# Squares of the differential-attention heads moved from ScalarE to GpSimd, and the item drains from VectorE to ScalarE

## The chip, the cores and the metric

One core of a Trainium2 chip runs the whole program. The metric is the device time of one execution in microseconds (us); lower is better. The engines are TensorE (PE in the profile), VectorE (DVE), ScalarE (ACT), GpSimd (POOL) and SyncE (SP, which issues DMA transfers). Each engine runs its instructions in program order; they wait for each other by counting semaphores.

## The reference

The program is one inference step of a two-layer decoder trunk for a prompt of 512 tokens and 8 x 4 decode tokens. The part touched here belongs to layer 1, differential attention with 6 heads of 128 value channels. For each head two score matrices are made, each has its softmax, and

```python
a = p[:, :, 0] - lam * p[:, :, 1]
return jnp.einsum('bhqk,bkhe->bqhe', a.astype(v.dtype), v)
...
o = rmsnorm(o, p['subln'][j]) * (1.0 - lam_init)
```

So each row (query token) of each head's output `o` is divided by the root of the mean of its 128 squares. The sum of those 128 squares is the statistic that the change is about. `o` then goes through `w_out`, and the MLP follows.

## The kernel before

**The items.** The prompt attention of layer 1 is cut into items `("diff", h, i)`: head h (0 to 5) and query tile i (0 to 3, 128 query rows each); the number of a tile is k = 4h + i. Tile i sees (i+1)*128 keys. Between the 24 of them stand four `decode` items, each for two of the eight decode requests, so that the head loop has 28 steps. Counted from its start, the decode items are items 8, 12, 17 and 23; k = 0 to 7 are items 0 to 7, k = 8 to 10 are 9 to 11, k = 11 to 14 are 13 to 16, k = 15 to 19 are 18 to 22, and k = 20 to 23 are 24 to 27.

**The stages of an item n**, by engine:
- PE `scores(n)`: query by key matmuls into PSUM, then a bf16 mask matmul (L725, L728). A decode item has L738 and L745 and reads keys from `cache_tiles`.
- DVE `items_bias(n)`: row maximum (L1635), then the bias of the exponential (L1639).
- ACT `items_exp(n)`: two exponentials with row sums (L1169).
- DVE `items_weight(n)`: reciprocal of the sums (L1607), ratio (L1615), and the weighted difference of the two probability tiles (L1617, a scalar_tensor_tensor with two SBUF inputs).
- PE `turn(n)`: transposes (L768). ACT `items_copy(n)`: PSUM to SBUF (L1183). PE `mix(n)`: by the values, into PSUM bank 7 (L806; L816 for decode).
- DVE `items_drain(n)`: bank 7 times the reciprocal into `O[:, k, :]` ("attention_out", L1661). A decode item goes ACT copy (L1215), PE `decode_turn` (L836), DVE copies (L1667).
- POOL: clamps the tile into one of two halves of `SQ[:, 0]` (L2121). ACT `items_square(n)`: the square of the clamped tile and the square of the tile scaled by 2^-68, both with the row sum as accumulator (L1193, L1195), into `ss` and `ss_big`. The scaled sum serves to recognise rows too large for the plain one.

**The order.** It is written out by hand, one function `attention` per engine, and each is a loop over steps n:
- PE step n: `scores(n+2)`, `decode_turn(n-2)` if it is one, `turn(n)`, `mix(n-1)`. `mix(n)` waits for `copied` of n and for `drained` of n-1, since bank 7 is used by every item. At step 26 the transposes of heads 0 and 1 (`turn_head`, L852) stand ahead of `turn(26)`.
- DVE step n: `items_weight(n)`, `items_drain(n-2)`, `items_bias(n+2)`; at steps 14 and 18 also the low part of a weight tile (L1400).
- ACT step n: `items_exp(n+1)`, the decode copy of n-2, `items_copy(n)`, `items_square(n-3)`; at steps 14 and 18 the high part of a weight tile (L1021).
- Heads 0 to 3 are finished inside the loop: the means at DVE step 22, the square root at ACT step 23 (L1224, with a load of the activation table ahead of it and another one for the next exponential), and at DVE step 24 the factors (L1681, L1682) and four `scale_head` (L1687). ACT loads the Sqrt table again at step 27 (L1208).
- Heads 4 and 5 are finished behind the loop, where DVE works through `means`, `head_factors`, `scale_head` and `head_rest` (L1889) before PE can do the rest of the output projection (L978).

**The cache tiles.** SP loads keys and values of a decode item with four 384 KB transfers each (L497). The values of the next decode item wait for `mixed` of the one before, which `decode_turn` increments; the keys of the one after next stand behind them in SP's queue.

## Time and profile before

| | us |
|---|---|
| three runs | 1254.06, 1259.02, 1259.39; median 1259.02 |
| profiled execution, first to last instruction (its span) | 1251.9 |
| PE busy | 1177.3 (94%) |
| DVE busy | 849.9 (68%) |
| ACT busy | 516.0 (41%) |
| POOL busy | 432.9 (35%) |

For the profiled execution no time of its own is given beside the span. Busy times are sums over the whole span; the head loop is only the stretch from about 714 to 796 us of it, and has other shares. PE busy includes matmuls whose ends are modelled.

### The profile page before, as it was taken

How to read it: one execution, taken by the hardware profiler on the slowest of the kernel's cores; microseconds unless marked ns; L12 is line 12 of the kernel's file. 1: busy time of each engine (PE TensorE's matmuls, PEld its weight loads, DVE VectorE, ACT ScalarE, POOL GpSimd, SP SyncE). 2: the span in 40 equal slices, each digit the busy share in tenths (PEclk: the TensorE clock that was granted, in tenths of full speed). 3: DMA queues.
4: the chain of work that ended last, by engine and by line, in shares of the span. 5: the costliest groups of instructions: out<-in, count | busy, mean ns of one | idle time of the engine just before them, and what ended most of it. 6: DMA issues, size and time to landing. Idle time of an engine off the chain costs nothing.

```text
span 1251.9 us, 23862 instructions
## 1 busy us (share of the span) xinstructions
PE 1177.3 (94%) x9338; PEld 1124.8 (90%) x9338; DVE 849.9 (68%) x1332; ACT 516.0 (41%) x1013; POOL 432.9 (35%) x332
## 2 busy tenths in 40 slices
PE   6998998999999999999999998798999999999996
PEld 6877888899999999999899855697999999999996
DVE  7667568776776767556643887667967767677634
ACT  7445334443343434334422277534434434333321
POOL 3363014453443444221036210011634434444312
PEclk9999999999999999999999999999899999999997
DMA  7632321322323223423255276022223232232302
GB/s 286 215 119 67 132 85 51 118 85 99 104 68 118 85 75 118 146 68 102 96 146 138 94 261 243 1 84 61 94 87 113 72 118 85 69 117 85 103 33 72
DMA packets 46229, 134.96 MB, mean 108 GB/s; under 512 B 4178, under 2 KB 6354, under 8 KB 45490
## 3 DMA queue, kind: packets, MB, share of 16 engines
q1 hardware_dynamic: 45026, 125.39, 30.0%
q0 software_dynamic: 1104, 8.15, 2.1%
q8 instruction: 74, 1.21, 0.4%
q14 instruction: 25, 0.20, 0.0%
HBM read 123.15 MB, written 7.03 MB: 104 GB/s over the span
## 4 chain that ended last, share of the span: by engine, by line
PE 70%; DVE 13%; ACT 6%; POOL 5%; issue 3%; DMA 2%; SPq 0%; ACTq 0%; DVEq 0%; POOLq 0%
PE psum L640 30%; PE psum L622 23%; PE psum L556 11%; DVE weights_split L1400 3%; ACT weights_split L1021 2%; ACT squares L1033 1%; DVE inv_rms L1421 1%; DMA rotated<-keys 1%; DMA rotated<-projected 1%; DVE residual L1425 1%; POOL projected L2089 1%; POOL projected L2090 1%; PE psum L711 1%; POOL rotated L2088 1%; PE psum L806 1%
## 5 line engine op out<-in xcount | busy, mean ns | idle before, releaser
L640 PE MATMUL psum<-operand_b,weights_split 128*128 128x272 f32 x1536 | 196.8, 289 | 2.2 <-DVE weights_split L1489 1.9
L640 PE MATMUL psum<-operand_a,weights_split 128*128 128x272 f32 (+1 forms) x1536 | 196.6, 289 | 1.9 <-DVE weights_split L1489 1.9
L640 PEld LDWEIGHTS psum<-operand_b,weights_split 128*128 128x128 f32 x1536 | 195.1, 190 | 2.6 <-DVE weights_split L1489 2.2
L640 PEld LDWEIGHTS psum<-operand_a,weights_split 128*128 128x128 f32 x1536 | 195.0, 190 | 2.2 <-DVE weights_split L1489 2.2
L556 PE MATMUL psum<-operand_b,weights_split 128*128 128x272 f32 x1344 | 177.0, 292 | 6.3 <-DVE weights_split L1400 6.1
L556 PEld LDWEIGHTS psum<-operand_b,weights_split 128*128 128x128 f32 x1344 | 171.3, 190 | 12.2 <-DVE weights_split L1400 8.0
L556 PE MATMUL psum<-operand_a,weights_split 128*128 128x272 f32 (+1 forms) x948 | 128.4, 294 | 20.6 <-DVE weights_split L1400 16.6
L556 PEld LDWEIGHTS psum<-operand_a,weights_split 128*128 128x128 f32 x948 | 122.1, 193 | 27.3 <-issue 16.5
L1400 DVE TENSOR_TENSOR weights_split<-weights_raw,weights_split 128x1024 fp32r<-128x1024 f32 (+1 forms) x66 | 86.4, 1309 | 45.9 <-ACT weights_split L1021 45.9
L1971 POOL TENSOR_TENSOR mem_keys<-weights_raw 128x512 f32<-128x512 f32 x28 | 39.7, 1419 | 212.4 <-DMA weights_raw<-in_weights 212.4
L1021 ACT ACTIVATE weights_split<-weights_raw 128x1024 fp32r<-128x1024 f32 (+1 forms) x66 | 66.3, 1004 | 91.8 <-PE psum L556 90.6
L1489 DVE TENSOR_TENSOR weights_split<-weights_raw,weights_split 128x1024 fp32r<-128x1024 f32 x64 | 91.7, 1435 | 9.2 <-ACT weights_split L1092 9.2
L1501 DVE TENSOR_TENSOR residual<-psum,residual 128x544 f32<-128x544 f32 x63 | 45.6, 723 | 67.8 <-PE psum L640 67.7
L622 PE MATMUL psum<-mixed_tokens,up_weights_a 128*128 128x272 f32 x672 | 89.2, 289 | 0.0
L622 PEld LDWEIGHTS psum<-mixed_tokens,up_weights_a 128*128 128x128 f32 x672 | 86.4, 188 | 0.0
L1993 POOL TENSOR_TENSOR operand_b<-staging,operand_b 128x544 fp32r<-128x544 f32 x32 | 53.6, 1692 | 82.3 <-ACT staging L1097 82.2
L1955 POOL TENSOR_TENSOR squares_sum<-squares_sum,squares 128x544 f32<-128x544 f32 (+1 forms) x35 | 47.7, 1364 | 98.7 <-ACT squares L1033 98.1
L1993 POOL TENSOR_TENSOR operand_a<-staging,operand_a 128x544 fp32r<-128x544 f32 x32 | 53.7, 1694 | 81.0 <-ACT staging L1097 80.9
L1477 DVE TENSOR_TENSOR up_weights_a<-weights_raw,up_weights_a 128x512 fp32r<-128x512 f32 x56 | 80.4, 1435 | 1.2 <-ACT up_weights_a L1079 1.2
L1092 ACT ACTIVATE weights_split<-weights_raw 128x1024 fp32r<-128x1024 f32 x64 | 67.1, 1048 | 17.2 <-PE psum L640 17.2
L1495 DVE TENSOR_TENSOR residual<-psum,residual 128x544 f32<-128x544 f32 x64 | 46.0, 718 | 37.0 <-PE psum L640 36.9
L1079 ACT ACTIVATE up_weights_b<-mem_values 128x512 fp32r<-128x512 f32 x28 | 17.7, 632 | 109.8 <-POOL mem_values L1984 109.8
(288 smaller groups left out, 2065.9 us busy)
## 6 DMA issues: line engine op xcount, KB each, us to landing
weights_raw<-in_weights SPq DMA_DIRECT2D x186, 512.0 KB, 3.7
cache_tiles<-in_page_k SPq DMA_DIRECT2D x16, 384.0 KB, 4.0
cache_tiles<-in_page_v SPq DMA_DIRECT2D x16, 384.0 KB, 4.1
cache_tiles<-in_mem_k SPq DMA_DIRECT2D x8, 512.0 KB, 4.5
cache_tiles<-in_mem_v SPq DMA_DIRECT2D x8, 512.0 KB, 5.1
residual<-in_x SPq DMA_DIRECT2D x1, 2176.0 KB, 12.8
rotated<-projected POOLq DMA_DIRECT2D x4, 408.0 KB, 7.2
rotated<-keys POOLq DMA_DIRECT2D x4, 408.0 KB, 7.0
```

The lines of the kernel that those rows point to most:

```text
L556: mm = pe.matmul(ps[:, 2 * (j % PS) + hf, 0:n], w(wr), act[:, ar, k, hf * n:(hf + 1) * n], start=(q == 0 and wr == 0 and ar == 0), stop=(q ...
L622: mm = pe.matmul(up_bank(UP_BANK[q]), up_split(q)[:, wr, lo_of(kk)], up_tokens(h2, q, ar, kk), start=(kk == 0 and wr == 0 and ar == 0), st ...
L640: mm = pe.matmul(ps[:, bank, 0:part.stop - part.start], w(wr), hidden[:, ar, 4 * (c % 2) + kk, part], start=(kk == 0 and wr == 0 and ar == 0),
L1021: act.activation(split[:, s % HL, 0, 0:n], raw[:, s, 0:n], ACT.Copy).then_inc(weight_hi, 1)
L1092: act.activation(split[:, d % HL, 0, :], raw[:, u % RAW, :], ACT.Copy).then_inc(weight_hi, 1)
L1400: dve.tensor_tensor(split[:, s % HL, 1, 0:n], raw[:, s, 0:n], split[:, s % HL, 0, 0:n].bitcast(F32), ALU.subtract).then_inc(weight_lo, 1)
L1477: ins = dve.tensor_tensor(at[:, 1, :], up_source(q, u % RAW), at[:, 0, :].bitcast(F32), ALU.subtract)
L1489: dve.tensor_tensor(split[:, d % HL, 1, :], raw[:, u % RAW, :], split[:, d % HL, 0, :].bitcast(F32), ALU.subtract).then_inc(weight_lo, 1)
L1495: dve.tensor_tensor(halves(X[:, k, :]), ps[:, 0:2, 0:HALF], halves(X[:, k, :]), ALU.add)\
L1501: dve.tensor_tensor(halves(X[:, k, :]), ps[:, 2:4, 0:HALF], halves(X[:, k, :]), ALU.add)\
L1955: pool.tensor_tensor(sq_sum[:, 0:cols], a, SQ[:, k % 2, 0:cols], ALU.add).then_inc(sq_summed, 1)
L1993: pool.tensor_tensor(hidden[:, 1, k, :], T[:, c, :], hidden[:, 0, k, :].bitcast(F32), ALU.subtract).then_inc(hid_lo, 1)
```

## The change

ScalarE now drains all `diff` items: `head_drain(n-2)` stands in ACT's step n between `items_exp(n+1)` and `items_copy(n)`, and behind the Sqrt table load of step 27. DVE drains only the decode items. For k = 0 to 19 POOL does the squares in five instructions per tile: clamp; scale by 2^-68; square of both at once (128x256); and two folding additions, of 2x64 and of 2x32 columns. The last leaves 2x32 partial sums per tile in `SQ[:, 1]`, and DVE adds them up for a whole head with one tensor_reduce of 2x4x32 elements, five steps behind the head's last item. For k = 20 to 23 (head 5) ACT still squares. `EARLY_DONE` grows by one, which puts the means of heads 0 to 3 at DVE step 23, the square root at ACT step 24, and factors and `scale_head` at DVE step 25.

```diff
+SQUARED = QT * (HEADS - 1)
...
+        stat_pairs = tiny[:, 16:160].rearrange("p (q k) -> p q k", q=2)
+        def square_pair(k):
+            return SQ[:, 0, 2 * P * (k % 2):2 * P * (k % 2) + 2 * P].rearrange("p (q c) -> p q c", q=2)
+        def head_sums(h):
+            at = 2 * P * (h % 2)
+            return SQ[:, 1, at:at + 2 * P].rearrange("p (q i c) -> p q i c", q=2, i=QT)
...
-        EARLY_DONE = FIRST_HEAD + ITEMS[FIRST_HEAD:].index(("diff", EARLY_HEADS - 1, QT - 1)) + 3
+        EARLY_DONE = FIRST_HEAD + ITEMS[FIRST_HEAD:].index(("diff", EARLY_HEADS - 1, QT - 1)) + 4
+        HEAD_LAST = [FIRST_HEAD + ITEMS[FIRST_HEAD:].index(("diff", h, QT - 1)) for h in range(HEADS)]
...
 ScalarE
             def items_square(n):
                 kind, a, i = ITEMS[n]
+                if kind == "diff" and QT * a + i >= SQUARED:
...
+            def head_drain(n):
+                kind, a, i = ITEMS[n]
                 if kind == "diff":
-                    k = QT * a + i
-                    act.wait_ge(clamped, k + 1)
-                    if k:
-                        act.wait_ge(squared, k)
-                    own.step(act.activation(SQ[:, 1, 0:P], SQ[:, 0, k % 2 * P:k % 2 * P + P], ACT.Square,
-                                            accum_out=ss[:, k:k + 1]))
-                    act.activation(SQ[:, 1, P:2 * P], O[:, k, :], ACT.Square, scale=BIG,
-                                   accum_out=ss_big[:, k:k + 1]).then_inc(squared, 1)
+                    act.wait_ge(mixed, n + 1)
+                    act.wait_ge(weighted, n + 1)
+                    act.activation(O[:, QT * a + i, :], ps[:, 7, 0:P], ACT.Copy, scale=coef[:, n % SLOTS, 0:1])\
+                       .then_inc(drained, 1)
...
+                    if n0 <= n - 2 < n1:
+                        head_drain(n - 2)
...
 VectorE
-                elif kind == "diff":
-                    s = n % SLOTS
-                    ins = dve.tensor_scalar(O[:, QT * a + i, :], ps[:, 7, 0:P], coef[:, s, 0:1], None, ALU.mult)
...
-                    if n - 2 >= n0:
+                    if n - 2 in DECODE:
                         items_drain(n - 2)
...
+                    if n - 5 in HEAD_LAST[:HEADS - 1]:
+                        h = HEAD_LAST.index(n - 5)
+                        dve.wait_ge(squared, QT * h + QT)
+                        dve.tensor_reduce(stat_pairs[:, :, QT * h:QT * h + QT], head_sums(h), AX.X, ALU.add)\
+                            .then_inc(head_summed, 1)
                     if n == EARLY_DONE + 1:
-                        dve.wait_ge(squared, EARLY)
+                        dve.wait_ge(head_summed, EARLY_HEADS)
...
-            dve.wait_ge(squared, QT * HEADS)
+            dve.wait_ge(head_summed, HEADS - 1)
+            dve.wait_ge(last_squared, QT * HEADS - SQUARED)
...
 GpSimd
                     k = QT * a + i
+                    pair = square_pair(k)
                     pool.wait_ge(drained, n + 1)
...
-                    pool.tensor_scalar(SQ[:, 0, k % 2 * P:k % 2 * P + P], O[:, k, :], CLAMP, -CLAMP, ALU.min, ALU.max)\
-                        .then_inc(clamped, 1)
+                    ins = pool.tensor_scalar(pair[:, 0, :], O[:, k, :], CLAMP, -CLAMP, ALU.min, ALU.max)
+                    if k >= SQUARED:
+                        ins.then_inc(clamped, 1)
+                    else:
+                        own.step(ins)
+                        own.chain(pool.tensor_scalar(pair[:, 1, :], O[:, k, :], BIG, 1.0, ALU.mult, ALU.mult))
+                        own.chain(pool.tensor_tensor(pair, pair, pair, ALU.mult))
+                        own.chain(pool.tensor_tensor(pair[:, :, 0:64], pair[:, :, 0:64], pair[:, :, 64:P], ALU.add))
+                        if a >= 2 and i == 0:
+                            pool.wait_ge(head_summed, a - 1)
+                        pool.tensor_tensor(head_sums(a)[:, :, i, :], pair[:, :, 0:32], pair[:, :, 32:64], ALU.add)\
+                            .then_inc(squared, 1)
```

## Rows read from the trace of the kernel before

**Rows 1.** Stretches: length; busy of PE, PEld, DVE, ACT, POOL; PEclk; DMA share; GB/s

```profile
714.00:723.00 9.00, 6.10 (x39) 3.24 (x38) 7.50 (x23) 6.85 (x25) 4.78 (x17) 1.00 0.99 350
...
728.00:741.00 13.00, 12.39 (x165) 8.16 (x164) 9.65 (x30) 10.04 (x45) 1.17 (x4) 1.00 0.53 186
741.00:754.00 13.00, 11.15 (x86) 6.89 (x82) 9.64 (x38) 9.07 (x38) 0.88 (x3) 1.00 0.74 243
754.00:767.00 13.00, 11.68 (x118) 6.57 (x116) 10.06 (x28) 9.52 (x38) 1.17 (x4) 1.00 0.73 244
767.00:780.00 13.00, 11.57 (x115) 8.15 (x117) 11.68 (x45) 8.87 (x39) 1.17 (x4) 1.00 0.76 273
780.00:790.00 10.00, 6.27 (x47) 3.20 (x48) 8.15 (x24) 8.39 (x26) 0.38 (x2) 1.00 0.04 16
```

**Rows 2.** Chain of waits, 706 to 812: start, duration, what

```profile
720.84 0.26 DVE attention_out L1661
...
745.54 3.81 DMA cache_tiles<-in_page_v
...
764.49 0.39 ACT squares L1193 x2
764.88 0.29 ACT squares L1195 x2
```

**Rows 3.** Groups by line and shape, 706 to 800: busy us, mean ns, idle before

```profile
L1661 DVE TENSOR_SCALAR attention_out<-psum,tiny 128x128 f32<-128x128 f32 x24 | 8.3, 347 | 2.8 <-PE psum L806 2.5
...
L1193 ACT ACTIVATE squares<-squares 128x128 f32<-128x128 f32 x24 | 7.2, 301 | 0.2
...
L1193 ACT ACTIVATION_READ_ACCUMULATOR squares<-squares 128x1 f32 x24 | 4.6, 192 | 0.0
...
L1635 DVE TENSOR_REDUCE tiny<-psum 128x2 f32<-128x256 f32 x6 | 2.5, 417 | 0.5 <-PE psum L728 0.5
...
L1183 ACT ACTIVATE staging<-psum 128x128 f32<-128x128 f32 x6 | 1.7, 277 | 2.8 <-PE psum L768 2.8
```

**Rows 4.** Groups of POOL by shape, whole span

```profile
L2121 POOL TENSOR_SCALAR squares<-attention_out 128x128 f32<-128x128 f32 x24 | 7.0, 292 | 68.5 <-DVE attention_out L1661 65.6 <-ACT squares L1195 2.9
...
L1955 POOL TENSOR_TENSOR squares_sum<-squares_sum,squares 128x544 f32<-128x544 f32 x29 | 43.1, 1488 | 96.7 <-ACT squares L1033 96.7
...
L1955 POOL TENSOR_TENSOR squares_sum<-squares_sum,squares 128x256 f32<-128x256 f32 x6 | 4.6, 764 | 2.0 <-ACT squares L1033 1.4
```

**Rows 5.** Timeline of DVE and POOL, 211 to 222 (MLP); last, L1617's ns minimum/median/maximum

```profile
212.40 1.77 DVE L1477 TENSOR_TENSOR up_weights_a<-weights_raw,up_weights_a 128x512 fp32r<-128x512 f32 x1
...
214.73 0.67 DVE L1477 TENSOR_TENSOR up_weights_a<-mem_keys,up_weights_a 128x512 fp32r<-128x512 f32 x1
...
211.57 2.06 POOL L1980 TENSOR_TENSOR weights_raw<-weights_raw 128x512 f32<-128x512 f32 x1
...
L1617 DVE SCALAR_TENSOR_TENSOR probs_heads<-probs_heads,tiny x15: 352/485/752, 718.0 to 788.9; 128x256 f32<-128x256 f32 x5, 128x384 f32<-128x384 f32 x4, 128x128 f32<-128x128 f32 x3, 128x512 f32<-128x512 f32 x3
```

**Rows 6.** Timeline of the end of the head loop, 782 to 794

```profile
782.08 0.24 DVE L1681 RECIPROCAL tiny<-tiny 128x16 f32<-128x16 f32 x1
...
782.57 2.50 DVE L1687 TENSOR_TENSOR attention_out<-attention_out,tiny 128x512 f32<-128x512 f32 x4
...
785.52 0.50 ACT L1215 ACTIVATE staging<-psum 128x384 f32<-128x384 f32 x1
...
788.44 0.17 DVE L1607 RECIPROCAL tiny<-tiny 128x2 f32<-128x2 f32 x1
...
790.03 0.17 DVE L1607 RECIPROCAL tiny<-tiny 128x2 f32<-128x2 f32 x1 [0.20 <-ACT staging L1169]
...
790.72 1.28 ACT L1208 ACT_TABLE_LOAD   x1
...
792.12 0.58 ACT L1183 ACTIVATE staging<-psum 128x512 f32<-128x512 f32 x1
...
793.21 1.13 PE L806 MATMUL psum<-values,staging 128*128 128x128 f32 x8 [0.54 <-DVE attention_out L1661]
```

More of the change, by code:

```diff
@@ L277, in build @@
         mixed, drained = sem("mixed"), sem("drained")
-        squared, clamped = sem("squared"), sem("clamped")
+        squared, clamped, last_squared = sem("squared"), sem("clamped"), sem("last_squared")
+        head_summed = sem("head_summed")
         new_mixed, new_added = sem("new_mixed"), sem("new_added")
@@ L969, in _ @@
             turn_head(3)
-            pe.wait_ge(squared, QT * HEADS + 1)
+            pe.wait_ge(last_squared, QT * HEADS - SQUARED + 1)
             pe.matmul(ps[:, 1, 0:NS], ones[:, :], SQ[:, 0, 0:NS], start=True, stop=True)
@@ L1187, in items_square @@
                 kind, a, i = ITEMS[n]
-                if kind == "diff":
-                    k = QT * a + i
-                    act.wait_ge(clamped, k + 1)
-                    if k:
-                        act.wait_ge(squared, k)
-                    own.step(act.activation(SQ[:, 1, 0:P], SQ[:, 0, k % 2 * P:k % 2 * P + P], ACT.Square,
-                                            accum_out=ss[:, k:k + 1]))
-                    act.activation(SQ[:, 1, P:2 * P], O[:, k, :], ACT.Square, scale=BIG,
-                                   accum_out=ss_big[:, k:k + 1]).then_inc(squared, 1)
+                if kind == "diff" and QT * a + i >= SQUARED:
+                    k = QT * a + i
+                    act.wait_ge(clamped, k - SQUARED + 1)
+                    if k > SQUARED:
+                        act.wait_ge(last_squared, k - SQUARED)
+                    own.step(act.activation(SQ[:, 1, 2 * P:3 * P], square_pair(k)[:, 0, :], ACT.Square,
+                                            accum_out=ss[:, k:k + 1]))
+                    act.activation(SQ[:, 1, 3 * P:4 * P], O[:, k, :], ACT.Square, scale=BIG,
+                                   accum_out=ss_big[:, k:k + 1]).then_inc(last_squared, 1)
+            def head_drain(n):
+                kind, a, i = ITEMS[n]
+                if kind == "diff":
+                    act.wait_ge(mixed, n + 1)
+                    act.wait_ge(weighted, n + 1)
+                    act.activation(O[:, QT * a + i, :], ps[:, 7, 0:P], ACT.Copy, scale=coef[:, n % SLOTS, 0:1])\
+                       .then_inc(drained, 1)
             def head_high(h):
@@ L1358, in _ @@
             act.wait_ge(sub_mean, 2)
-            act.wait_ge(squared, QT * HEADS)
+            act.wait_ge(head_summed, HEADS - 1)
+            act.wait_ge(last_squared, QT * HEADS - SQUARED)
             own.step(act.activation(SQ[:, 0, 0:NS], small[0], ACT.Square))
             act.activation(SQ[:, 1, 0:NS].rearrange("p (h t) -> p h t", h=MIXT), Z[:, 0:MIXT, PROMPT:TOK], ACT.Square,
-                           scale=BIG).then_inc(squared, 1)
+                           scale=BIG).then_inc(last_squared, 1)
             act.wait_ge(sub_mean, 3)
@@ L2117, in _ @@
                     k = QT * a + i
+                    pair = square_pair(k)
                     pool.wait_ge(drained, n + 1)
-                    if k >= 2:
+                    if k >= SQUARED + 2:
+                        pool.wait_ge(last_squared, k - SQUARED - 1)
+                    elif k >= 2:
                         pool.wait_ge(squared, k - 1)
-                    pool.tensor_scalar(SQ[:, 0, k % 2 * P:k % 2 * P + P], O[:, k, :], CLAMP, -CLAMP, ALU.min, ALU.max)\
-                        .then_inc(clamped, 1)
+                    ins = pool.tensor_scalar(pair[:, 0, :], O[:, k, :], CLAMP, -CLAMP, ALU.min, ALU.max)
[10 more added lines that the diff above has]
+                            .then_inc(squared, 1)
             sum_squares(R_MLP1)
```

## The prediction, written before the changed kernel was run

> **What bounds the kernel now.** I read first the busy time by stretch of the head loop [rows 1], then its chain of waits [rows 2], then the costs of the instructions that go or come [rows 3, 4], and last the timeline of the loop's end [rows 6], since the change moves work between steps there. Outside this loop the change touches nothing.
>
> In the six stretches shown PE is busy for 12.39 of 13 us at best and 6.27 of 10 at worst; its idle time is 2.90 + 0.61 + 1.85 + 1.32 + 1.43 + 3.73 = 11.8 us [rows 1]. PE is therefore the nearest to a bound, no edit on DVE or ACT can be worth more than these 11.8 us, and the reader should look for what ends each of those idle times. ACT has 6.85 to 10.04 us busy in 9 to 13, DVE 7.50 to 11.68: neither is full over a whole stretch but the two take turns in holding PE up. DVE's drain stands in the chain for 0.26 us at 720.84 and four times more behind (at 756.50, 758.60, 773.64, 792.71); ACT's squares stand in it with 0.39 + 0.29 = 0.68 us at 764.49 [rows 2]. The stretch from 741 to 754 is held by something else: the value tiles of the second decode item, the last of which needs 3.81 us to land, at 749.35 [rows 2]. Their issue waits for the transpose of the first decode item, and the keys of the third are issued behind them, so from 741 to about 754 a faster ACT or DVE gives nothing, for all of PE's 1.85 idle us.
>
> **What goes.** From DVE 24 drains of 0.347 us, 8.3 us [rows 3]. From ACT the squares of 20 tiles: two activations of 0.30 and two reads of the accumulator of 0.19 each, 0.98 us busy a tile, 20 x 0.98 = 19.7 us [rows 3], of which 0.68 us a tile shows in the chain because they overlap [rows 2]. Following the chain, what it gives back is: 0.26 at 720.84; 0.25 at 756.50 (there PE has the third decode item's scores to finish, so the squares ahead at 752.9 give nothing more); 0.26 at 758.60; 0.68 at 764.49, where ACT's squares, its weight tile and its exponential stand in line; 0.26 at 773.64. Sum 1.7 us. The other 19 pairs of squares lie beside time in which ACT waits for PE's transposes anyway.
>
> **What ACT gets.** 24 drains. The trace has no PSUM-to-SBUF activation with a scale of this shape; the plain copy of 128x128 takes 0.277 us [rows 3], and DVE's own drain, which has the scale, 0.347; I take 0.30, with these as the ends, 6.6 to 8.3 us in all. Inside the loop they stand ahead of `items_copy(n)`, which mostly waits for PE: nothing, except at the end (below). `mix(n-1)` and POOL wait for them.
>
> **What DVE gets.** Five reductions of 256 elements, 0.417 us by the nearest row, which reads PSUM [rows 3]; 2.1 us. They stand behind `items_bias(n+2)` at steps 8, 12, 18, 23 and 27, where DVE next waits for ACT or PE; the second lies in the stretch held by the DMA. I take 0, with 2.1 as the other end. Each waits for POOL: queued behind it is `items_weight(n+1)`, and PE's transposes wait for that.
>
> **What POOL gets.** Per tile a clamp and a scale of 0.292, a square of 128x256 at 0.764, and folds of 128 and 64 elements. From 256 to 544 elements the addition grows from 0.764 to 1.488 us, 2.5 ns an element [rows 4]; so 0.44 and 0.28. Sum 2.07 us, and with four hand-overs from one instruction to the next, some 0.07 us each as an estimate, 2.35. Tiles 0 to 7 are drained within 15.8 us, one every 2.25 us, so POOL is at the loop's own pace there and about 1 us behind after eight. The reduction of a head comes five steps behind its last item, three steps (some 7 us) behind its drain. POOL is not late; a wait there costs 0.
>
> **The shared resource.** While POOL's L1980 ran until 213.63, a DVE subtraction with two SBUF inputs, started at 212.40, took 1.77 us; the same shape with POOL idle took 0.67 at 214.73 [rows 5]. So such a DVE instruction waits for the end of POOL's. In the head loop every diff item has one, L1617, of 0.35 to 0.75 us [rows 5], and the small L1639 too. Now POOL is busy there for about 1 us in 13 [rows 1]; afterwards for most of the time. An instruction that arrives at random while POOL works waits for half the running one, weighted by length: (2 x 0.29² + 0.76² + 0.44² + 0.28²) / (2 x 2.07) = 0.25 us. In the chain stand seven L1617 before 780, of which I find five at a time when POOL will be at work: 5 x 0.25 = 1.2 us. The ends: 0, if POOL always finds itself the one that waits, and 48 x 0.25 = 12 us if all of both kinds were in the chain.
>
> The Trainium skill, "SBUF — State Buffer", section "Who interferes with whom", says that a DVE instruction with two SBUF inputs contends with a GpSimd instruction that reads SBUF, and that the second to issue is fully blocked until the first ends. By that rule the trace agrees: 1.77 against 0.67 us. A rule of proportional sharing would leave the weights late by a tenth of a microsecond and the sum some 0.7 us lower; the full block speaks against the change, because the order of issue and not the priority decides.
>
> **The end of the loop.** Here something is moved, and this decides the sign. Factors and four `scale_head` take from 782.08 to 784.99, 2.9 us [rows 6]. Before, they stand at step 24, in the time when DVE waits for ACT's decode copy (785.52) anyway, which comes behind the square root, its two table loads and two exponentials. Afterwards they stand at step 25, behind `items_bias(27)`, directly ahead of `items_weight(26)`. The decode copy comes at the same time as before: what ACT saves in squares it loses in waiting for `turn(24)` before it can start the square root. So `items_weight(26)` starts not at 788.44 but at 791.35. Before, 0.20 us of wait for the exponential lay ahead of `items_weight(27)` at 790.03 [rows 6]; now it follows at 791.35 + 1.13 = 792.48: 2.45 us later. PE's transposes of heads 0 and 1 lie beside that and give nothing.
>
> ACT adds to this. Its Sqrt table load at 790.72 lies before in the wait for `turn(27)`, and the copy starts at 792.12 [rows 6]. Now it starts only when the copy of item 26 is through, 793.6, and it and its activation last 1.4 us; then drain 25 (0.3) and the copy of 27. `mix(26)` waits for drain 25 until 795.3. Drain 26 stands behind copy 27 and the squares of tile 20 (0.8), and ends at 796.9; `mix(27)` starts at 797.0 instead of 793.21 [rows 6]: 3.8 us later, the above 2.45 included. Behind the loop drain 27, two pairs of squares and `head_high` on ACT make DVE's means 0.4 us later still. Sum 4.2 us. What follows is a line of DVE work and then PE without gaps: the delay stays.
>
> **Sum.** -1.7 + 1.2 + 4.2 = +3.7 us: the span goes from 1251.9 to 1255.6. The span is all that is known of the profiled execution; it is 7.1 us under the median of the runs shown, 1259.02, whose own spread is 5.3 us. I add the 3.7 to the median: 1262.7.
>
> **Rivals.**
> - (A) The relief of ACT carries further than the chain shows, since with ACT early the exponentials, and so the weights, run ahead. For it: PE's idle time of 2.90, 1.32 and 1.43 us in stretches without the DMA. Against it: DVE is 7.5 of 9 and 11.7 of 13 us busy in two of them. It would give all 5.7 us of these and no blocking; with the 4.2 us of the end, -1.5: 1257.5. If `scale_head` also found cover, 2.45 less: 1255.
> - (B) Blocking decides. If POOL, slowed by DVE in turn (0.35 to 0.75 us once a tile, to about 2.9 us against a pace of 2.25), keeps a backlog, L1617 meets a busy POOL every time and DVE becomes the bound from its first tile: it loses 0.3 us a drain and gains 0.5 us a tile, and the reductions begin to wait. 20 tiles x 0.25 to 0.5 in the chain are 5 to 10 us: -1.7 + 7 + 4.2 = +9.5, 1268.5. It decides from about 2.7 us of POOL per tile. Against it: the pauses of POOL at each decode item (7 to 9 us between drains) clear the backlog.
> - (C) The end costs nothing, because ACT, free of squares, does the square root before `turn(24)` would stop it: -0.5 us in all, 1258.5. Against it is only ACT's order, which is fixed.
>
> **How the numbers follow.** Forecast 0.50, its own range 1260 to 1266; A 0.17, B 0.18, C 0.15. The range of eight in ten, with the runs' own scatter of 5 us: 1255 to 1269.5. Half a per cent, 6.3 us, is what a measurement of this kernel can tell from no change. Beyond it on the slow side lie most of B and a tail of the forecast: 0.24. On the fast side only a lucky A with scatter: 0.10. The rest 0.66.
>
> **What would show it.** Right: four L1687 directly ahead of L1617 with 384 keys, DVE without a gap there; the table load of L1208 behind the last but one copy and not in a wait; PE's gap ahead of the last two `mix` longer; L1617 with a maximum above 0.9 us; 741 to 754 of unchanged length; POOL at 2.3 to 2.6 us a tile. Wrong: no waits of DVE for POOL and a loop up to the first square root shorter by more than 3 us (A), or POOL above 2.7 us a tile and DVE waiting at the reductions (B), or the decode copy 2 us earlier (C).

## The result, and the profile after

| | us |
|---|---|
| changed kernel, median of five runs | 1261.2 (1260.36 to 1263.95) |
| kernel before beside it, median of six runs | 1254.2 (1253.0 to 1259.39) |
| ratio, with its 95% interval | 1.0046 [1.0028, 1.0063] |
| profiled execution of the changed kernel | 1263.95, span 1262.2 |

A sixth run of the changed kernel, 1902 us, was disturbed and is left out. The ratio compares runs taken side by side: the change costs 0.46%, 5.8 us, with an interval from 3.5 to 7.9; forecast were 3.7, just inside it. The profiled execution is the slowest of the five, so its span exaggerates: 10.3 us over the span before.

The stretches of the changed kernel's head loop, with the columns of [rows 1]:

```profile
714.00:723.00 9.00, 6.02 (x32) 3.36 (x34) 6.97 (x20) 7.36 (x27) 5.71 (x19) 0.89 0.98 337
...
728.00:741.00 13.00, 11.97 (x118) 8.01 (x117) 10.47 (x27) 8.16 (x29) 9.16 (x22) 1.00 0.53 187
...
767.00:780.00 13.00, 11.24 (x115) 6.20 (x111) 10.02 (x29) 8.04 (x24) 7.78 (x17) 1.00 0.60 210
...
790.00:796.00 6.00, 2.66 (x14) 2.29 (x15) 4.44 (x14) 2.91 (x9) 0.63 (x1) 0.73 0.00 0
796.00:805.00 9.00, 6.86 (x29) 5.52 (x27) 2.71 (x8) 4.25 (x15) 0.59 (x2) 0.50 0.01 3
805.00:815.00 10.00, 10.00 (x51) 9.94 (x52) 6.37 (x18) 5.69 (x19) 0.29 (x1) 0.59 0.00 0
```

ACT has less to do (8.16 against 10.04 us in 728 to 741, 8.04 against 8.87 in 767 to 780) and POOL much more (9.16 against 1.17), as the change says. PE did not profit: its idle time in 767 to 780 is 1.76 us against 1.43 [rows 1]. New is the column PEclk in the last three rows: the granted clock is 0.73, 0.50 and 0.59 there. The kernel before has in its own last stretches:

```profile
790.00:796.00 6.00, 4.77 (x39) 4.26 (x38) 2.33 (x7) 5.58 (x21) 1.08 (x4) 1.00 0.01 3
796.00:805.00 9.00, 7.17 (x56) 6.71 (x54) 8.69 (x22) 4.71 (x11) 0.00 (x0) 1.00 0.00 0
```

The timeline of the changed kernel's end of the loop, answering to [rows 6] (start, duration; in brackets the idle time before it and who ended it). L1711 is now the `scale_head` line, L1634 the reciprocal of `items_weight`, L1666 was L1639, L1644 was L1617, L821 was L806, L851 was L836 (`decode_turn`), L1241 was L1215, L867 is `turn_head`, L859 the matmuls of the new tokens, L1219 is ACT's new drain:

```profile
786.29 1.28 ACT L1250 ACT_TABLE_LOAD   x1
...
787.91 1.28 ACT L1184 ACT_TABLE_LOAD   x1
...
790.34 0.49 ACT L1241 ACTIVATE staging<-psum 128x384 f32<-128x384 f32 x1
...
790.88 0.55 PE L851 MATMUL psum<-constants,staging 128*128 128x128 f32 x3 [2.21 <-ACT staging L1241]
...
793.16 0.16 DVE L1666 SCALAR_TENSOR_TENSOR tiny<-tiny 128x2 f32<-128x2 f32 x1
793.24 0.24 DVE L1705 RECIPROCAL tiny<-tiny 128x16 f32<-128x16 f32 x1
...
793.72 2.59 DVE L1711 TENSOR_TENSOR attention_out<-attention_out,tiny 128x512 f32<-128x512 f32 x4
...
794.56 1.94 PE L867 MATMUL psum<-constants,attention_out 128*128 128x128 f32 x8 [1.96 <-DVE attention_out L1711]
...
796.24 0.15 DVE L1634 RECIPROCAL tiny<-tiny 128x2 f32<-128x2 f32 x1
...
798.85 1.28 ACT L1232 ACT_TABLE_LOAD   x1
...
800.75 1.62 PE L821 MATMUL psum<-values,staging 128*128 128x128 f32 x6 [0.68 <-ACT attention_out L1219]
...
802.92 2.04 PE L821 MATMUL psum<-values,staging 128*128 128x128 f32 x8 [0.55 <-ACT attention_out L1219]
...
804.89 2.77 PE L859 MATMUL psum<-probs_new,values_new 32*128 32x32 f32 x12
```

The reader should see three things. The four `scale_head` stand where they were forecast: directly behind L1666 and directly ahead of `items_weight(26)`, with no gap on DVE. The table load of step 27 follows the copy of item 26 (798.35) and not a wait. And PE waits 2.21 + 1.96 us between 788.7 and 794.6, after which the last `mix`, eight matmuls that took 1.13 us before [rows 6], takes 2.04. Only the second of these waits is new. The first was there before, in the same place:

```profile
786.08 0.55 PE L836 MATMUL psum<-constants,staging 128*128 128x128 f32 x3 [2.29 <-ACT staging L1215]
```

The groups of the new and lengthened instructions in the changed kernel, 706 to 812 (busy us, mean ns, idle before):

```profile
L2160 POOL TENSOR_TENSOR squares<-squares 128x256 f32<-128x256 f32 x20 | 13.4, 670 | 1.7
L2161 POOL TENSOR_TENSOR squares<-squares 128x128 f32<-128x128 f32 x20 | 10.9, 544 | 1.6
L1219 ACT ACTIVATE attention_out<-psum,tiny 128x128 f32<-128x128 f32 x24 | 8.7, 363 | 2.7 <-PE psum L821 2.6
L2154 POOL TENSOR_SCALAR squares<-attention_out 128x128 f32<-128x128 f32 x24 | 7.7, 320 | 34.6 <-ACT attention_out L1219 33.8
...
L2164 POOL TENSOR_TENSOR squares<-squares 128x64 f32<-128x64 f32 x20 | 7.3, 367 | 1.6
...
L2159 POOL TENSOR_SCALAR squares<-attention_out 128x128 f32<-128x128 f32 x20 | 6.0, 300 | 1.6
...
L1666 DVE SCALAR_TENSOR_TENSOR tiny<-tiny 128x2 f32<-128x2 f32 x24 | 4.7, 196 | 0.8
...
L1644 DVE SCALAR_TENSOR_TENSOR probs_heads<-probs_heads,tiny 128x512 f32<-128x512 f32 x3 | 3.0, 1015 | 0.1
...
L1729 DVE TENSOR_REDUCE tiny<-squares 128x8 f32<-128x256 f32 x5 | 2.1, 412 | 0.0
```

**Where the time went, by milestones.** So that executions can be compared, each profile is cut at four starts on its own timeline: the loop's first exponential (714.83 before), PE's `decode_turn` of the third decode item (767.46) and of the fourth (786.08), the matmuls of the new tokens behind the last `mix` (794.27), and ACT's instruction that writes `operand_a` from `projected` (L1371 before, 804.52). The stretches between them, in us:

| kernel | to third turn | to fourth turn | to new tokens | to end | sum |
|---|---|---|---|---|---|
| before | 52.6 | 18.6 | 8.2 | 10.3 | 89.7 |
| changed | 56.2* | 20.0 | 14.0 | 12.3 | 102.5 |
| changed again (run 9) | 52.9 | 20.0 | 14.0 | 11.9 | 98.8 |
| 1 move alone | 54.6* | 19.1 | 13.0 | 11.5 | 98.2 |
| 2 changed, not moved | 53.0 | 21.3 | 10.5 | 11.5 | 96.4 |
| 3 drains alone | 53.9 | 20.9 | 11.0 | 12.4 | 98.2 |
| 4 POOL squares alone | 53.1 | 19.1 | 8.8 | 10.3 | 91.2 |
| 5 filled | 55.5* | 20.0 | 12.0 | 10.4 | 98.0 |
| 6 Sqrt load behind | 53.1 | 20.0 | 13.4 | 10.6 | 97.1 |
| 7 POOL reads | 54.4 | 19.4 | 8.2 | 10.2 | 92.3 |
| 8 POOL writes | 54.4* | 18.8 | 10.2 | 11.5 | 94.8 |
| 10 filled again | 54.4* | 20.0 | 12.0 | 10.4 | 96.8 |
| 11 split drains | 53.1 | 18.4 | 9.3 | 10.7 | 91.5 |
| 12 one table load | 53.0 | 18.0 | 9.9 | 12.1 | 93.0 |

In the rows with a star the granted clock is below 1.00 in part of 714 to 728, for instance 0.51 in 721 to 728 of the changed kernel. This befalls kernels with and without any part of the change (1 has the same code there as the kernel before, and 8 its work and order) and is absent when the changed kernel is profiled again. So the first column of a starred row says nothing of an edit. Between the unstarred rows of before and of run 9 lie +0.3, +1.4, +5.8 and +1.7 us. Their sum, 9.2, is larger than the difference of the medians, 6: run 9's profile (1262.69) lies 1.8 us above the median of its kernel, and that of before about 1 us under its own. (Its span is 1251.9; in the other profiles the time is some 1.8 us over the span, so as an estimate it took 1253.7, against 1254.81.)

### The profile page after: what moved, and what is told of

The parts are those of the page before. It is cut to its first block, busy times and chain, and to the rows that moved or that the text cites. A ratio compares the mean times of both kernels' runs of the same rounds, so it can differ in the third digit from the quotient of the medians.

```text
span 1262.2 us, 23875 instructions
## 1 busy us (share of the span) xinstructions
PE 1185.1 (94%) x9338; PEld 1129.5 (89%) x9338; DVE 847.7 (67%) x1313; ACT 511.9 (41%) x957; POOL 471.4 (37%) x412
## 4 chain that ended last, share of the span: by engine, by line
PE 69%; DVE 13%; ACT 6%; POOL 5%; issue 4%; DMA 2%; SPq 0%; DVEq 0%; ACTq 0%; POOLq 0%
PE psum L655 29%; PE psum L637 22%; PE psum L571 10%; DVE weights_split L1427 3%; ACT weights_split L1036 2%; ACT squares L1048 1%; PE psum L821 1%; DVE inv_rms L1448 1%; DVE residual L1452 1%; POOL projected L2119 1%; DMA rotated<-projected 1%; DMA rotated<-keys 1%; POOL projected L2120 1%; PE psum L726 1%; POOL rotated L2118 1%
## 5 line engine op out<-in xcount | busy, mean ns | idle before, releaser
L1036 ACT ACTIVATE weights_split<-weights_raw 128x1024 fp32r<-128x1024 f32 (+1 forms) x66 | 66.3, 1005 | 91.5 <-PE psum L571 91.3
```

The source lines that it names most:

```text
L1036: act.activation(split[:, s % HL, 0, 0:n], raw[:, s, 0:n], ACT.Copy).then_inc(weight_hi, 1)
```

## The experiments

Each ran in five rounds beside the kernel before; those of one group shared a chip and its runs of before, whose medians were 1255.5 (kernels 1 to 4), 1253.78 (5 to 8) and 1254.81 (9 to 12).

**1. The move alone**: the kernel before with

```diff
-        EARLY_DONE = ... + 3
+        EARLY_DONE = ... + 4
```

> The kernel before with one edit: EARLY_DONE one larger, so that the means of heads 0 to 3 stand at DVE step 23, the square root at ACT step 24, factors and scale_head at DVE step 25. Nothing moves between engines. Theory M (the moved scale_head is most of the loss): 3 to 6 us slower than before, 1.0025 to 1.005, with the four L1687 directly ahead of the weight of item 26 and a gap of PE ahead of it. Rival P (the loss is POOL's work blocking DVE): within 1 us of before.

Measured 1259.84, ratio 1.0034 [1.0018, 1.0049]. Without a new instruction on any engine, 4.3 us. The windows of its profile:

```profile
790.00:796.00 6.00, 4.90 (x21) 4.37 (x22) 4.71 (x12) 2.52 (x6) 0.59 (x2) 0.50 0.01 3
796.00:805.00 9.00, 8.47 (x37) 7.91 (x37) 3.12 (x12) 5.68 (x24) 0.59 (x2) 0.50 0.00 0
```

and its timeline:

```profile
789.45 2.50 DVE L1687 TENSOR_TENSOR attention_out<-attention_out,tiny 128x512 f32<-128x512 f32 x4
...
790.28 1.94 PE L852 MATMUL psum<-constants,attention_out 128*128 128x128 f32 x8 [1.94 <-DVE attention_out L1687]
...
797.60 2.05 PE L806 MATMUL psum<-values,staging 128*128 128x128 f32 x8 [0.53 <-DVE attention_out L1661]
```

It shows the same picture as the changed kernel: `scale_head` ahead of the weights, PE idle for 1.94 us, and the clock at half level behind.

**2. The changed kernel without the move**

```diff
-        EARLY_DONE = ... + 4
+        EARLY_DONE = ... + 3
...
-                    if n - 5 in HEAD_LAST[:HEADS - 1]:
+                    if n - 4 in HEAD_LAST[:HEADS - 1]:
```

> The changed kernel with the move taken back: EARLY_DONE as before (+3) and every head reduction four steps behind the head's last item instead of five. Theory M: the loss of 5.8 to 7.8 us shrinks to 0 to 3 us, with the decode copy of item 23 about where it stands in the changed kernel and the last mix 2.5 to 6 us earlier. Rival P: still 5 us or more slower than before. If POOL is late for the earlier reductions, DVE waits on L2164 ahead of its reduction and the time is over that of the changed kernel.

Measured 1257.88, 1.0027 [1.0011, 1.0043]. It should have been near the kernel before if the move were the whole cost; it is 3.4 us slower. Its timeline names the reason:

```profile
779.34 1.28 ACT L1250 ACT_TABLE_LOAD   x1
...
780.64 0.31 ACT L1250 ACTIVATE tiny<-tiny 128x16 f32<-128x16 f32 x1
...
780.96 1.28 ACT L1184 ACT_TABLE_LOAD   x1
...
783.17 0.36 ACT L1219 ACTIVATE attention_out<-psum,tiny 128x128 f32<-128x128 f32 x1
...
783.63 2.21 PE L831 MATMUL psum<-cache_tiles,staging 128*32 128x384 f32 x15 [2.46 <-issue]
```

The fourth decode item's `mix` (L831) needs bank 7 empty, and so the drain of the item before it. With DVE that drain was through at once. On ACT it stands at step 24 behind the two table loads, the square root and the two exponentials of item 25, and ends at 783.53. "issue" in the bracket is misleading: the profile shows no releaser, but PE resumes 0.1 us after ACT's drain. So the drains on ACT need the move, at least that of item 22 (experiment 11), and the move has the price of experiment 1.

**3. The drains alone**: the kernel before with `head_drain` on ACT as in the diff of the change, DVE draining decode items only; ACT keeps its squares, nothing is moved.

> The kernel before with the 24 drains of the diff items moved from DVE to ACT and nothing else; ACT keeps all squares. ACT then has 8.7 us more and is the fuller engine. Theory M (drains stand beside waits, except behind the table load of step 27): +1 to +2 us, all of it in the last 10 us of the loop. Rival D (the drains on ACT hold up PE's mix all through the loop): +4 us or more, spread over the stages.

Measured 1261.38, 1.005 [1.0033, 1.0067], 6 us slower: the smaller of the two expectations fails. The timeline shows the same wait as in 2, ahead of the same matmuls, although nothing of POOL's part is in this kernel:

```profile
786.67 2.79 PE L816 MATMUL psum<-cache_tiles,staging 128*32 128x384 f32 x16 [2.93 <-issue]
```

ACT's drain of item 22 ends 0.1 us ahead of it, as in 2. But the loss is not in one place: against the profile of before the four stretches are longer by 1.3, 2.3, 2.8 and 2.1 us. To that extent rival D's expectation (spread over the stages) fits better, for a kernel in which ACT has the drains and still all its squares; what holds it up outside the wait was not followed.

**4. POOL's squares alone**: the changed kernel with the drains back on DVE and nothing moved.

```diff
-        EARLY_DONE = ... + 4
+        EARLY_DONE = ... + 3
...
-                    if n0 <= n - 2 < n1:
-                        head_drain(n - 2)
...
+                elif kind == "diff":
+                    s = n % SLOTS
+                    ins = dve.tensor_scalar(O[:, QT * a + i, :], ps[:, 7, 0:P], coef[:, s, 0:1], None, ALU.mult)
...
-                    if n - 2 in DECODE:
+                    if n - 2 >= n0:
                         items_drain(n - 2)
...
-                    if n - 5 in HEAD_LAST[:HEADS - 1]:
+                    if n - 4 in HEAD_LAST[:HEADS - 1]:
```

> The kernel before with the squares of 20 tiles on POOL and the head reductions on DVE (four steps behind), while DVE keeps the drains and scale_head stays where it was before. Theory M with blocking at 1.2 us in the chain: -1 to +1.5 us. Rival P (blocking decides): +4 us or more, with L1617's longest over 1 us and its mean of 512 columns up from 0.75 by 0.2 or more.

Measured 1253.97, 0.9987 [0.9969, 1.0004]: no difference that can be told. The 19.7 us of ACT work that leave are worth between nothing and 4 us, after what POOL's squares and DVE's reductions take back.

**5. PE kept busy**: the changed kernel with matmuls of a tile of ones into free banks, six ahead of the fourth `decode_turn`, six ahead of the transposes of head 0 and two ahead of `turn(26)`. Their products are not read.

```diff
+                    if n == n1 - 3:
+                        pe.wait_ge(exped, n1 - 2)
+                        for _ in range(6):
+                            pe.matmul(ps[:, 2, 0:P], ones[:, :], ones[:, :], start=True, stop=True)
...
```

> The changed kernel with 14 idle-time matmuls of ones by ones (128x128 f32) on PE, into PSUM banks that are free then: 6 ahead of decode_turn of item 23, 6 ahead of turn_head(0) and 2 ahead of turn(26), where PE stood still for 2.2, 2.0 and 0.9 us. They compute nothing that is used. Theory C (PE's idle time there is followed by a fall of the granted clock to half, in the changed kernel 20 us of it from about 793 us on, and this costs 3 to 5 us of the loss): the clock stays at full in the stretch 790 to 805, the last two mix take 0.83 and 1.13 us again instead of 1.62 and 2.04, and the time comes 3 to 4.5 us under that of the changed kernel, +1.5 to +4.5 us against before. Rival N (the fall comes where it comes): the same as the changed kernel or up to 1 us slower, with the half clock in place.

Measured 1259.71, 1.0045 [1.0028, 1.0062]. The windows of its profile:

```profile
790.00:796.00 6.00, 4.16 (x33) 3.38 (x32) 4.14 (x14) 3.21 (x11) 0.56 (x1) 1.00 0.01 3
796.00:805.00 9.00, 5.85 (x45) 4.97 (x44) 3.24 (x9) 5.94 (x22) 0.95 (x4) 1.00 0.00 1
805.00:815.00 10.00, 7.96 (x61) 7.38 (x60) 9.65 (x24) 5.17 (x14) 0.00 (x0) 1.00 0.00 0
```

Locally it did what was meant: full clock throughout, and the last two columns of the table are together 3.9 us shorter than the changed kernel's (run 10 against run 9: 3.5). The median did not follow.

**6. The Sqrt table load of step 27 behind the last copy**

```diff
-                    if n == n1 - 1:
-                        own.step(act.activation(tiny[:, 13:14], epsc, ACT.Sqrt))
...
                     if n < n1:
                         items_copy(n)
+                    if n == n1 - 1:
+                        own.step(act.activation(tiny[:, 13:14], epsc, ACT.Sqrt))
```

> The changed kernel with the Sqrt table load of ACT's step 27 behind items_copy(27) instead of ahead of head_drain(25). Nothing else. Theory (the table load stands in the path of drain 25 and of the last copies for 1.4 us): then drain 25 and copy 27 come 1.4 us earlier but drain 26 stays where it is, behind load and squares, so the last mix moves by 0.5 us or less; 0 to -1 us against the changed kernel. Rival (all 1.4 us and a longer full clock come back): -2 us or more against the changed kernel.

Measured 1259.68, 1.0043 [1.0028, 1.0058]. Its table load starts at 798.17 and the drain of item 26 behind it at 800.16; PE's last `mix` waits 1.85 us for that drain where it waited 0.55. The load only changed places with the wait it causes, as was expected.

**7 and 8. What a busy POOL costs DVE.** Both are the kernel before with four additional POOL instructions a tile, on memory that nothing reads. In 7 they are those of the change and read SBUF; in 8 they are memsets of about the same lengths, which only write.

```diff
 (7)
+                    if k < QT * (HEADS - 1):
+                        pool.wait_ge(clamped, k + 1)
+                        own.chain(pool.tensor_scalar(SQ[:, 0, 3 * P:4 * P], ..., BIG, 1.0, ALU.mult, ALU.mult))
+                        own.chain(pool.tensor_tensor(..., ALU.mult))
+                        own.chain(pool.tensor_tensor(..., ALU.add))
+                        own.chain(pool.tensor_tensor(..., ALU.add))
 (8)
+                    if k < QT * (HEADS - 1):
+                        pool.wait_ge(clamped, k + 1)
+                        for cols in (243, 650, 480, 290):
+                            own.chain(pool.memset(spare[:, 0:cols], 0.0))
```

> The kernel before, all its work and order kept, with four more POOL instructions behind each clamp of the first 20 tiles, of the shapes of the changed kernel (scale 128x128, square 128x256, folds of 128 and 64), on a spare part of the tile of squares; nobody waits for them. This is the price of POOL's presence alone. Theory (blocking is real but mostly beside the path): 0 to +2 us, L1617 of 512 columns with a maximum over 1.0 us and L1639 with a maximum over 0.4. Rival P: +4 us or more.

> As the run with POOL reads, but the four POOL instructions of each tile are memsets of about the same lengths (243, 650, 480 and 290 columns), which read nothing. If DVE's instructions with two SBUF inputs wait only for POOL instructions that read, L1617 and L1639 keep their 0.752 and 0.160 us at most and the time is that of before. If any POOL instruction blocks them, they look as in the run with reads.

Measured 1255.16, 1.001 [0.9991, 1.0028], and 1255.02, 0.9997 [0.9982, 1.0013]. The ratios differ by 0.0013, 1.6 us, less than either interval is wide. The groups decide. Of 7:

```profile
L1639 DVE SCALAR_TENSOR_TENSOR tiny<-tiny 128x2 f32<-128x2 f32 x24 | 5.4, 227 | 0.8
...
L1617 DVE SCALAR_TENSOR_TENSOR probs_heads<-probs_heads,tiny 128x512 f32<-128x512 f32 x3 | 2.6, 874 | 0.1
```

Of 8, where these two lines are one further down:

```profile
L2127 POOL MEMSET spare<- 128x650 f32 x20 | 12.8, 640 | 1.1
...
L1640 DVE SCALAR_TENSOR_TENSOR tiny<-tiny 128x2 f32<-128x2 f32 x24 | 4.1, 170 | 0.8
...
L1618 DVE SCALAR_TENSOR_TENSOR probs_heads<-probs_heads,tiny 128x512 f32<-128x512 f32 x3 | 2.3, 751 | 0.1
```

751 ns is the duration before (the maximum in [rows 5] is 752). POOL is as long at work in both, and only where it reads does the DVE instruction with two SBUF inputs get longer, by 0.12 us in the mean. The Trainium skill, "SBUF — State Buffer", section "Who interferes with whom", says that such a DVE instruction contends with a GpSimd instruction that reads SBUF and not with one that only writes it; these two runs agree.

The profile of 8 shows something else, which matters for the clock:

```profile
790.00:796.00 6.00, 5.39 (x26) 4.76 (x27) 3.97 (x10) 4.70 (x15) 0.59 (x2) 0.57 0.00 0
796.00:805.00 9.00, 8.46 (x39) 7.91 (x38) 3.73 (x13) 5.64 (x23) 0.59 (x2) 0.53 0.01 2
```

This kernel has the order of the kernel before, nothing moved, PE's one long wait there (2.29 us), and the median of the kernel before. Still its granted clock is at half level for some 14 us from 790.5 on, and its last two stretches are 3.2 us longer. One profile with a low clock at the loop's end is therefore no proof that an edit brought it.

**9 and 10. The changed kernel and the filled one again**, side by side, to see whether the clock's local gain is real in the median.

> The changed kernel once more, for comparison on one chip with the next three: 1.003 to 1.006 of before. If the half clock behind PE's idle time at the loop's end belongs to this kernel and is no accident of one execution, its profile again has more than 10 us of it between 790 and 815 us.

> The changed kernel with the 14 idle-time matmuls once more, beside the changed kernel itself. Theory C (the fall of the clock at the end of the loop costs 3 to 5 us net): 2.5 us or more under the changed kernel. Rival N (the local gain is real but falls of the clock come elsewhere in its place, so that little is left): within 1.5 us of the changed kernel, with full clock from 780 to 815.

Measured 1260.9, 1.0055 [1.0034, 1.0075], and 1260.5, 1.0048 [1.0027, 1.007]. The windows of 9:

```profile
790.00:796.00 6.00, 2.97 (x13) 2.09 (x11) 5.75 (x18) 2.09 (x6) 0.63 (x1) 0.54 0.00 0
796.00:805.00 9.00, 7.75 (x32) 6.80 (x33) 1.40 (x4) 5.63 (x20) 0.88 (x3) 0.50 0.01 3
```

and of 10:

```profile
790.00:796.00 6.00, 3.40 (x26) 2.65 (x25) 3.99 (x10) 3.04 (x8) 0.92 (x2) 1.00 0.00 1
796.00:805.00 9.00, 8.45 (x56) 7.99 (x55) 4.97 (x16) 6.22 (x26) 0.58 (x2) 0.81 0.00 0
```

Again the filled kernel keeps the clock for most of the end (it is at half level for 3.4 us there, against 20.5 in 9), and again its median is the same as that of the changed one within what can be told (the ratios differ by 0.0007). The profiled execution of 10 took 1254.76 us, the shortest of its nine, whose median is 1260.5: a single profile can show a gain that the runs do not have. The median fits rival N's expectation, but not its reason: the clock did not fall elsewhere in its place, since the mean granted clock of the nine executions is 0.985 and that of the six of experiment 9 is 0.981.

**11. The drains split**: ACT drains tiles 0 to 18, DVE tiles 19 to 23, which are those behind and beside the table loads; nothing is moved, the squares are on POOL.

```diff
+        LATE_DRAIN = FIRST_HEAD + ITEMS[FIRST_HEAD:].index(("diff", 4, 3))
...
-                    if n0 <= n - 2 < n1:
+                    if n0 <= n - 2 < LATE_DRAIN:
                         head_drain(n - 2)
...
-                    if n - 2 in DECODE:
+                    if n - 2 in DECODE or (n - 2 >= LATE_DRAIN):
                         items_drain(n - 2)
```

> POOL squares as in the changed kernel, scale_head unmoved, head reductions four steps behind; ACT drains tiles 0 to 18, DVE drains tiles 19 to 23, whose drains would stand behind ACT's table loads. Theory T (drains on ACT cost only behind the table loads): within 1 us of the run where DVE does all drains, 0.998 to 1.0005 of before, and no wait of PE on L831 or L821 over 1 us. Rival D (drains on ACT hold PE all through the loop, 0.2 us or so each): 1.002 or more.

Measured 1253.59, 0.9992 [0.9977, 1.0007]. With 19 of 24 drains on ACT the loss is gone. In its timeline the fourth decode item's `mix` has no wait ahead of it, and the wait ahead of `decode_turn` is half as long:

```profile
782.93 1.50 PE L832 MATMUL psum<-cache_tiles,staging 128*32 128x384 f32 x16
...
786.83 0.55 PE L852 MATMUL psum<-constants,staging 128*128 128x128 f32 x3 [1.13 <-ACT staging L1242]
```

**12. One table load instead of three**: experiment 4 with the square root of heads 0 to 3 in the place of step 27's Sqrt, and their factors, `scale_head` and transposes at the loop's end or behind it.

> A version meant to beat both: POOL squares, DVE drains, and the square root of heads 0 to 3 in the place of the dummy Sqrt of ACT's step 27, so that two of the three table loads go (2.9 us with the root); factors and scale_head(0) follow at DVE step 28, the other three at step 29, the transposes of heads 0 and 1 and head_high(0) behind the loop. The loop then ends 2 to 3.5 us earlier, the DVE work behind it grows by 1.4 to 2.1 us. If that is all: -0.5 to -3 us against before. If the DVE line behind the loop takes all three scale_head and the wait for PE's transposes, +0 to +2 us.

Measured 1256.45, 1.0011 [0.9997, 1.0025], no gain. The fourth turn comes 1.2 us earlier than in 4 (71.0 against 72.2 us from the first exponential), but the new tokens' matmuls start at the same distance, 80.9 us, because the last `mix` takes 2.04 us instead of 1.13, and the transposes of four heads follow behind the loop as 3.54 us of PE.

## Why the prediction was right, and where it was not

**Right: the sign and the place; the size partly by luck.** +3.7 us was forecast and +5.8 measured, with 3.5 as the lower end of the interval. 1261.2 us lies in the likeliest case's own range of 1260 to 1266, but that rests on a start from 1259.02, the median of three runs; the six have 1254.2. A start 4.8 us too high and a change 2.1 us too small came out near the measured time together: from 1254.2 the same sum gives 1257.9, and 1261.2 stands at the upper end of its own range. The end of the loop is the place: the move alone costs 4.3 us (experiment 1), and with POOL's squares and 19 of the 24 drains but without the move nothing is lost that can be measured (experiment 11). But the move is not the only edit there that costs (experiments 2 and 3, below).

**The signs that were named.** The four L1687 directly ahead of the weights, the table load behind the copy, a longest L1617 above 0.9 us (1.15) and the unchanged length of 741 to 754 were all seen. PE's gap ahead of the last two `mix` is hardly longer: 0.68 and 0.55 us where there was none and 0.54. The new gap, 1.96 us, stands ahead of the transposes of head 0.

**The end of the loop, forecast +4.2.** From the fourth turn to the new tokens' matmuls the forecast was +3.8, and +0.4 behind them. With the clock at full level (run 5 throughout, run 10 but for 3.4 us) they are 12.03 - 8.19 = +3.84 and 10.38 - 10.25 = +0.13: the steps and their lengths were right. In the changed kernel itself they are +5.8 and +1.7 to 2.0. The difference, 3.5 us in run 9, is the term that the sum did not have: around PE's waits of 2.21 and 1.96 us the granted clock falls to 0.50, the lower of its two levels, 1.2 GHz, and six matmuls of `mix` take 1.62 us, eight take 2.04 and the twelve of the new tokens 2.77, where the filled kernel has 0.91 and 1.13 and the kernel before 1.52 for the twelve. I had forecast PE's longer gap and looked only at what it delays, not at what PE does when it resumes. The Trainium skill, "TensorE: Matmul & The Clock Gate", Part 1, describes a clock that is lowered by idleness between these same two levels. The traces agree on the levels, and with PE's gaps filled the clock stayed up (run 5); they do not single out the new gap. In run 9 the clock falls at 790.5, ahead of the second wait (791.5 to 793.2), and in run 8 it falls without one.

That the lower clock belongs to the change nevertheless is shown by all executions together, since the mean granted clock of each is known: 0.981 in the eleven of the changed kernel, 0.982 in experiments 1 and 3, against 0.985 in the 91 of the kernel before, 0.986 in the 21 of the filled kernel and 0.987 in experiments 4 and 11. Among those 91 a clock lower by 0.001 goes with 0.70 us more time; by that the missing 0.0044 is worth about 3 us, an estimate, and half of the loss. What stays open is why the filled kernel, at the clock of the kernel before, is still 5 to 6 us slower (1.0045 and 1.0048). Its matmuls give the clock back and something else takes the time; no profile shows what.

**The front, forecast -1.7.** This step failed: the relief in the chain was counted and did not come. Up to the third turn run 9 is +0.3, from there to the fourth +1.4. Even with the blocking of +1.2 subtracted, nothing of the 1.7 is seen. Two terms were too low. ACT's drain takes 0.363 us, above my upper end of 0.347: the copy whose 0.277 I leaned on has no per-row scale. The Trainium skill, "ScalarE: Activation LUTs", section "What ACT_TABLE_LOAD costs", gives about 93 ns for each per-partition operand of an activation. An estimate from it is 0.277 + 0.093 = 0.370 us, and the measured 0.363 agrees. The second is DVE's reductions, which I had put at zero because DVE would wait there anyway. At least two of the five stand in the chain. At step 18 this one follows DVE's part of a weight tile and ends ahead of `items_weight(19)`; PE then waits 0.64 us for that weight (run 9, at 770.68) where it waited 0.20:

```profile
769.45 0.41 DVE L1729 TENSOR_REDUCE tiny<-squares 128x8 f32<-128x256 f32 x1
```

From there on everything is 0.44 us later, counted from the third turn. At step 23 the last reduction (0.41) and the means, one of which takes 0.60 instead of 0.18, stand ahead of `items_weight(24)`; `turn(24)` waits 0.31 us for it, and the copy behind `turn(24)` is what the square root and both table loads wait for. That is 0.4 to 0.5 of the 1.4 us; the other 0.9 is there already at `turn(22)` (9.4 against 8.5 us behind the third turn): the 0.44 of step 18, and 0.4 from the 512-column L1644 ahead of it, which took 1.13 us instead of 0.75. "The decode copy comes at the same time as before" was therefore wrong by 1.4 us. The deeper error may be to add up single chain entries: where another releaser follows closely, taking 0.26 us away only moves the chain to the next engine. This was not tried entry by entry and is not shown. Experiment 4, which takes ACT's 19.7 us away and gives POOL and DVE the squares' work instead, gains 1.6 us with an interval that includes zero.

**The blocking, forecast +1.2.** Of the six L1644 with 512 columns three take 1.015 us in the mean instead of 0.752, and three still 0.752: +0.13, half of what I had worked out for one that arrives at random (in run 9 the three take 0.879). 7 against 8 prices POOL's reading at 1.6 us, not resolved. The backlog of rival B did not occur: POOL took 2.2 us busy and 2.76 from one tile's clamp to the next (721.48 to 724.24), at B's threshold of 2.7, but no reduction waited (0.0 idle before L1729) and over the whole loop L1644 is busy 1.4 us longer (14.6 against 13.2 in kernel 8) and L1666 0.8 us (4.7 against 3.9 before), so that at most 2.2 us are in the chain, not 5 to 10. My 2.07 for POOL missed the fold of 128 columns, 0.544 instead of 0.44, and that of 64, 0.367 instead of 0.28: a price worked out from 256 and 544 columns was too low for fewer. Why is not shown.

**What was not named: the coupling.** I took the move as a given part of the diff and asked only what it costs, and put the drains on ACT at nothing "except at the end", behind the table load of step 27. Experiments 1, 2 and 11 show that it belongs to the drains: on ACT the drain of item 22 falls behind the table loads (2, 2.46 us of PE's time), moved, it avoids that and pushes `scale_head` ahead of the weights (1). Either costs 3 to 4 us; leaving those few drains on DVE costs nothing (11).

**The stretch of the DMA** (741 to 754) kept its length: from the first decode item's turn (`decode_turn`) to the second's `mix` 8.75 us against 8.5 (8.6 in run 9), and PE's wait there, small as before, is for the cache tiles, as forecast:

```profile
753.38 1.50 PE L831 MATMUL psum<-cache_tiles,staging 128*32 128x384 f32 x16 [0.20 <-DMA cache_tiles<-in_page_v]
```

Rival A (5.7 us of relief and no blocking) is refuted by experiment 4, whose interval ends at 3.9 us of gain. Rival C said that ACT, free of squares, would do the square root before `turn(24)` stops it, and that the decode copy would come 2 us earlier; it came 1.4 us later. Experiment 1 is no test of C, since ACT keeps its squares there. No version tried beats the kernel before: the best, 4 and 11, have 0.9987 and 0.9992, both with 1 in the interval.

## What to carry to other kernels

Where two engines take turns in holding up a third, relief of one of them is worth what is left when its neighbour becomes the last, not the sum of its entries in the chain; here 19.7 us of ACT work, moved to POOL, were worth between nothing and 4. Before a drain is moved to the engine that also loads activation tables, look at what stands ahead of it at each table load, since a PSUM bank that is emptied late holds PE, and move only the drains that do not fall there. And price a longer gap of PE twice: what it delays, and at which clock the matmuls behind it run. To tell whether a low clock comes from an edit, compare the mean clock of many executions, not two profiles: here one profile of a kernel as fast as the one before had it too.

## What the runs showed of the hardware

- A POOL instruction lengthens DVE's instructions with two SBUF inputs if it reads SBUF, and not if it only writes: 751 ns with memsets beside, 874 with reading instructions of about the same length, 752 in the kernel before, where POOL is hardly at work.
- Around 2.2 and then 1.7 or 2.0 us of PE waiting, the granted clock went to half level and stayed there for 20.5 us in both profiles of the changed kernel; with matmuls in the gaps it was 1.00 in one profile, and 1.00, 0.81, 1.00 in the other. With the one wait of 2.3 us it stayed up in the profile of the kernel before and was at half level for 13.7 us in that of experiment 8.
- Over whole executions the mean granted clock is 0.981 for the changed kernel, 0.985 for the one before and 0.986 with the gaps filled.
- A low clock at the loop's start (0.51 in 721 to 728) comes and goes between executions of the same code, and goes with 1.5 to 3.3 us more in a single profile there.
- An ACT activation from PSUM of 128x128 takes 0.277 us without and 0.363 with a scale from SBUF.
